# A two-layer diffusion trunk on one core: adaLN steps moved into the first norm, final states moved to w_out's transposes, other PSUM banks for the second norm, attention's first values later

## The reference

```
mod = silu(cond) @ w_ada[l] + b_ada[l]          # 6 x 1024: sh1 sc1 g1 sh2 sc2 g2
hn  = rmsnorm(x, norm_mix) * (1 + sc1) + sh1
proj = hn @ w_in[l]                             # 3840 columns, three head groups
  differential attention (8 heads) | retention (4 heads, both directions) | HGRN2 (4 heads, both)
x  += g1 * (concat of the three @ w_out[l])
hn  = rmsnorm(x, norm_ffn) * (1 + sc2) + sh2
x  += g2 * moe(hn)                              # 16 experts, top 2, gate/up/down of 1024 x 512
```

## Time and profile before

| | us |
|---|---|
| median of 3 runs | 951.66 |
| the profiled execution, whole | 953.32 |
| its span, first to last instruction | 951.5 |
| PE busy | 920.2 |
| DVE busy | 431.9 |
| ACT busy | 158.7 |
| POOL busy | 63.7 |

### The profile page before, as it was taken

One profiled execution on the slowest core, in us unless ns is written; L12 is line 12 of the kernel. 1 busy time (PEld: TensorE's weight loads), 2 busy tenths in 40 slices (PEclk: granted clock), 3 DMA queues, 4 the chain that ended last, 5 costly groups with the idle time before them and its releaser, 6 DMA issues.

```text
span 951.5 us, 13385 instructions
## 1 busy us (share of the span) xinstructions
PE 920.2 (97%) x5191; PEld 499.6 (53%) x5197; DVE 431.9 (45%) x780; ACT 158.7 (17%) x408; POOL 63.7 (7%) x96
## 2 busy tenths in 40 slices
PE   5999999999999999999999999999999999999997
PEld 2755575568553444344437556657864444443442
DVE  1385887742423122232145999876252321222223
ACT  2212024320210100010111211432021001000100
POOL 1112230020000000000000223000000000000001
PEclk9999999999999999999999999999999999999999
DMA  9996574675999999999996632601189999999993
GB/s 365 401 390 268 222 267 177 243 278 213 408 420 422 421 421 421 421 422 420 421 421 252 225 124 91 235 32 38 35 364 422 421 421 421 421 421 421 421 421 137
DMA packets 48430, 303.63 MB, mean 319 GB/s; under 512 B 7680, under 2 KB 7696, under 8 KB 14960
## 3 DMA queue, kind: packets, MB, share of 16 engines
q1 hardware_dynamic: 42368, 291.52, 75.2%
q0 software_dynamic: 2960, 8.63, 2.6%
q10 hardware_dynamic: 3040, 2.62, 0.8%
HBM read 300.10 MB, written 2.65 MB: 318 GB/s over the span
## 4 chain that ended last, share of the span: by engine, by line
PE 84%; DVE 9%; DMA 3%; ACT 2%; issue 1%; SPq 0%; DVEq 0%; ACTq 0%
PE ps L427 82%; PE ps L461 2%; DMA ring<-in_w_in 2%; ACT eP L1582 1%; DMA ring<-in_w_ada 1%; DVE fa L1263 1%; DVE rt L1057 1%; DVE eP L1361 1%; DVE stat L1057 1%; DVE xy L1257 1%; DVE eP L1359 1%; DVE hnT L1105 0%; DVE sq L1214 0%; DVE proj L1290 0%; DVE proj L1224 0%
## 5 line engine op out<-in xcount | busy, mean ns | idle before, releaser
L427 PE MATMUL ps<-ring,proj 128*64 128x512 f32 x1024 | 226.3, 595 | 1.0 <-ACT proj L1829 1.0
L427 PE MATMUL ps<-ring,hnT 128*128 128x512 f32 (+1 forms) x576 | 203.2, 505 | 2.3 <-issue 1.2
L427 PEld LDWEIGHTS ps<-ring,hnT 128*128 128x128 f32 x576 | 106.9, 191 | 75.9 <-issue 67.7
L427 PEld LDWEIGHTS ps<-ring,proj 128*64 128x64 f32 x1024 | 72.6, 137 | 132.8 <-issue 131.1
L427 PE MATMUL ps<-hnT,ring 128*64 128x128 f32 (+2 forms) x576 | 74.0, 342 | 2.9 <-DVE hnT L1105 1.6
L427 PEld LDWEIGHTS ps<-hnT,ring 128*64 128x64 f32 (+1 forms) x576 | 60.7, 160 | 13.9 <-issue 2.9
L427 PEld LDWEIGHTS ps<-proj,xs 128*128 128x128 f32 x512 | 58.4, 192 | 12.5 <-issue 11.4
L427 PE MATMUL ps<-proj 128*128 128x512 f32 x128 | 61.7, 607 | 0.0
L427 PE MATMUL ps<-proj,xs 128*128 128x128 f32 x512 | 61.4, 278 | 0.1
L1553 DVE COPY proj<-ps 128x512 f32<-128x512 f32 x16 | 11.1, 692 | 108.0 <-PE ps L427 108.0
L427 PE MATMUL ps<-ring,silT 128*32 128x512 f32 x384 | 48.8, 630 | 9.6 <-DVE silT L1073 6.9
(11 more groups left out here) (231 smaller groups left out, 920.9 us busy)
## 6 DMA issues: line engine op xcount, KB each, us to landing
ring<-in_w_gate SPq DMA_DIRECT2D x64, 1024.0 KB, 14.4
ring<-in_w_down SPq DMA_DIRECT2D x64, 1024.0 KB, 16.8
ring<-in_w_ada SPq DMA_DIRECT2D x48, 1024.0 KB, 8.6
ring<-in_w_in SPq DMA_DIRECT2D x28, 1024.0 KB, 8.5
eP<-in_w_up SPq DMA_DIRECT2D x16, 1024.0 KB, 15.8
wT<-in_w_up SPq DMA_DIRECT2D x16, 1024.0 KB, 17.9
fa<-in_w_up SPq DMA_DIRECT2D x16, 1024.0 KB, 17.7
xy<-in_w_up SPq DMA_DIRECT2D x16, 1024.0 KB, 19.1
```

What stands on the lines that cost most here:

```text
L427: ins = nc.tensor.matmul(*a, **k)
```

## The change

Six edits, in both layers unless said otherwise:

1. `AT_CHANGE` becomes (5, 1, 1): layer 1 takes five adaLN steps before the norm of g = 0 as before, one after it, and one after the norm of g = 1. The two come from behind block r, where three stood and one stays. SP loads six of them before block f of layer 1 and the seventh behind f.
2. `da_values(0, 0)` moves behind the first half of block s.
3. The final state of the retention moves, in layer 1 only, ahead of the last adaLN steps and of the first `out_of`; the final state of HGRN2 moves in both layers from the second norm to the transposes of w_out, and uses bank 1 (`b = 2 - i`).
4. The second norm's g = 1 uses banks 2 and 0, not 0 and 3.
5. ACT's copies of the states move to match, and both states are stored before the second norm.
6. One semaphore, `stored`, counts all stores.

```diff
-ADA_BEHIND = ((2, 3, 3, 3, 3, 2, 3, 2), (0, 0, 0, 0, 0, 3, 0, 0))
-AT_CHANGE = 5
+ADA_BEHIND = ((2, 3, 3, 3, 3, 2, 3, 2), (0, 0, 0, 0, 0, 1, 0, 0))
+AT_CHANGE = (5, 1, 1)
...
-                    for step in IN_CHANGE:
+                    change = iter(IN_CHANGE)
+                    for step in itertools.islice(change, sum(AT_CHANGE[0:2])):
                         load_ada(*step)
...
+                    if l and name == "f":
+                        for step in change:
+                            load_ada(*step)
...
-                    b = claim_for_norm() if h or first is None else first
+                    if banks[h] is not None:
+                        b = banks[h]
+                        pe.wait_ge(S(f"bank{b}_free"), c.claim(b))
+                    else:
+                        b = claim_for_norm() if h or first is None else first
...
-                    normalized_group("hn1", "xn1", 0, at_change)
+                    normalized_group("hn1", "xn1", 0, lambda b: at_change(0))
+                    at_change(1)
...
                         if l and g:
                             normalized_group("hn1", "xn1", 1)
+                            at_change(2)
...
-                    b = 2
+                    b = 2 - i
...
-                da_values(0, 0)
 
                 ss = open_block("s")
                 b = by_token("s", 0, 0, ss)
+                da_values(0, 0)
...
                 transposed("mix", "mixed", 0, (6, 7))
+                if l:
+                    end_state(0, "r", T_RV)
                 ada_steps(len(LATER[l]))
...
                         transposed("mix", "mixed", 1)
-                        end_state(0, "r", T_RV)
+                        if not l:
+                            end_state(0, "r", T_RV)
+                        end_state(1, "h", T_GI)
                         copied_group("mix", 1)
...
                 normalized_group("hn2", "xn2", 0)
-                end_state(1, "h", T_GI)
                 if l + 1 < L:
-                    normalized_group("hn2", "xn2", 1, lambda b: next_layers(3))
+                    normalized_group("hn2", "xn2", 1, lambda b: next_layers(3), banks=(2, 0))
                 else:
-                    normalized_group("hn2", "xn2", 1, lambda b: stream_zeros(b, 5))
+                    normalized_group("hn2", "xn2", 1, lambda b: stream_zeros(b, 5), banks=(2, 0))
...
+                if l:
+                    end_state(0, "r")
                 mixed_columns(1)
-                end_state(0, "r")
+                if not l:
+                    end_state(0, "r")
+                end_state(1, "h")
                 store_state(0, "o_ret")
+                store_state(1, "o_hg")
                 squares("xn2")
-                end_state(1, "h")
...
-                store_state(1, "o_hg", "stored_state")
```

More of the change, by code:

```diff
@@ L335, in build @@
         LATER = [[(0, "g", k) for k in range(KC)] + [(0, "y", k) for k in range(KC)] + [(1, "x", k) for k in range(KC)],
-                 [(1, "y", k) for k in range(AT_CHANGE, KC)]]
+                 [(1, "y", k) for k in range(sum(AT_CHANGE), KC)]]
         IN_ROUTER = [(1, "g", k) for k in range(KC)]
-        IN_CHANGE = [(1, "y", k) for k in range(AT_CHANGE)]
+        IN_CHANGE = [(1, "y", k) for k in range(sum(AT_CHANGE))]
         half_experts = {n: ap[n].rearrange("l e h p m -> p (l e h) m") for n in ("w_gate", "w_up", "w_down")}
@@ L482, in claim_for_norm, with normalized_group @@
                 return b
-            def normalized_group(stage, factors, g, ahead=None, first=None):
+            def normalized_group(stage, factors, g, ahead=None, first=None, banks=(None, None)):
                 xv = x[:, g].rearrange("p (k q) -> p k q", k=KC)
                 for h in range(2):
-                    b = claim_for_norm() if h or first is None else first
+                    if banks[h] is not None:
[3 more added lines that the diff above has]
+                        b = claim_for_norm() if h or first is None else first
                     if not h:
@@ L549, in next_layers, with at_change @@
                         ada_step(*step)
-                def at_change(b):
-                    for step in IN_CHANGE:
+                change = iter(IN_CHANGE)
+                def at_change(n):
+                    for step in itertools.islice(change, AT_CHANGE[n]):
                         ada_step(*step)
@@ L1619, in squares, with store @@
                         rstd(g, slice(2, 3), D, (stage + "r", g))
-                def store(dst, src, name="stored"):
-                    acte.dma_start(dst, src).then_inc(S(name), 16)
-                    led.made(name, (name,), 16)
+                def store(dst, src):
+                    acte.dma_start(dst, src).then_inc(S("stored"), 16)
+                    led.made("stored", ("stored",), 16)
                 squares("xn1")
                 acte.wait_ge(S("stored"), c.before("stored"))
-                if l:
-                    acte.wait_ge(S("stored_state"), c.before("stored_state"))
                 def modulation(l, what, norm):
@@ L1739, in end_state, with store_state @@
                     evac((name + "state",), None, name + "stateS", fn=lambda src: nc.scalar.copy(stout[:, i].rearrange("p h e -> p (h e)"), src[:, 0:256]))
-                def store_state(i, out, name="stored"):
+                def store_state(i, out):
                     for d in range(2):
-                        store(ap[out][0].rearrange("l r h d e -> r d l h e")[d, :, one(l)].rearrange("d l h e -> d (l h) e"), stout[64 * d:64 * d + 64, i], name)
+                        store(ap[out][0].rearrange("l r h d e -> r d l h e")[d, :, one(l)].rearrange("d l h e -> d (l h) e"), stout[64 * d:64 * d + 64, i])
                 def ret_columns(a, to, scale):
@@ L1841, in _ @@
             acte.wait_ge(S("stored"), c.value("stored", "end", 0) + 32)
-            acte.wait_ge(S("stored_state"), c.value("stored_state", "end", 0))
         @block.gpsimd
```

## The result

The changed kernel takes 958.49 us (median of 12 runs, 957.01 to 961.31), the kernel before, run beside it, 953.70 us (12 runs, 950.55 to 956.13). The ratio is 1.0056, interval 1.0040 to 1.0073: 5.3 us slower, between 3.8 and 7.0. The direction was as forecast and the size near it (+4.3, inside that interval); the time itself, forecast at 956.0 in a range to 957.9, was not.

What follows compares the result with a forecast made beforehand. TensorE's chain was 84%, but a saturated load stream was met first. +3.0 at f (layer 0's 0.3 included), +0.3 block s, -0.5 second norm, +1.5 clock: +4.3 on 951.66 gives 956.0, range 953.6 to 957.9.

Steps and rivals of the forecast that it cites:

- f's place in the stream: Layer 1's first norm: f's second half lands one 1 MB load, 2.5 us, later; TensorE waits 2.5 to 3.4 us.
- The stream's late start: Layer 0's second norm: HGRN2 state delays the load stream 0.93 us, o_hg stores give back 0.1; f complete at 507.1.
- The clock at f: Block f of layer 1: the wait drops TensorE's clock to 0.5, priced at 1.5 us, ends 0 and 1.9.
- Two steps less behind r: Layer 1 behind block r: 1.8 us less TensorE only lengthens the wait at v's bank to about 3.0; value 0.
- Block s: Bank turn makes modulation_by_feature wait 1.3 us in layer 1; net +0.3 us per layer, no clock drop in layer 1.
- rival B: A second clock drop, at block s of layer 1 behind the new 1.3 wait: +1.2 us more, 957.2; chance 0.12.
- The second norm: Layer 1's second norm: moved state and freed bank together give -0.5 us, ends 0 and -0.93.
- The base: Whole kernel: the +4.3 us change is added to the median of 951.66, giving 956.0; the profiled execution took 953.32.
- DMA idle: Load stream: saturated from 240 to 503 us; DMA idle anywhere between 240 and 500 would show the forecast wrong.
- 0.25 us before its use: Block f of layer 1: its second half landed at 503.5, 0.25 us before f started at 503.75.

Runs made afterwards that it cites:

- a2: The changed kernel with (4, 1, 1), so five adaLN loads before f again, and two steps behind r: 955.17 us, ratio 1.0019 to the kernel before.
- c1: The changed kernel with eleven matmuls of zeros in the wait before block f of layer 1: 957.01 us, ratio 1.0041 to the kernel before.
- a1: The kernel before with only the moved adaLN steps and their loads, (5, 1, 1) and one step behind r: 957.39 us, ratio 1.0054.
- a3: The changed kernel with da_values(0, 0) back ahead of block s: 958.25 us, ratio 1.0049 to the kernel before.
- a4: The changed kernel with layer 0's HGRN2 state and its stores back between the second norm's groups, in bank 1: 959.17 us, ratio 1.0060 to the kernel before.
- b2: The changed kernel with eight matmuls of zeros ahead of the adaLN step behind block r in layer 1: 958.15 us, ratio 1.0046 to the kernel before.
- d1: The kernel before with da_values(0, 0) behind block s's first half, plus four matmuls of zeros before modulation_by_feature, both layers: 954.58 us, ratio 1.0008.
- b6: The kernel before with only da_values(0, 0) moved behind the first half of block s: 956.38 us, ratio 1.0022.
- b3: The changed kernel with (4, 1, 1), two steps behind r, da_values(0, 0) back, layer 0's HGRN2 state back in bank 2: 953.09 us, ratio 0.9985 to the kernel before.
- b4: The kernel before with edits 3 to 6 in layer 1 alone; second norm's banks (2, 0) and layer 0's state in bank 2: 952.35 us, ratio 0.9988.

## Why the prediction was right or wrong

**f's place in the stream: right.** The wait in front of f, forecast between 2.5 and 3.4 us, was 2.57, ended by the load, and 2.30 with edit 1 alone; it went with one load less (a2). f for g = 1 came 4.30 us later against the steps ahead of it; the forecast had 3.0 - 0.3 + 1.5 = 4.2. That it fits to 0.1 is partly luck: f started 2.87 later against the steps and not 3.1, and the clock cost 0.2 more than in the sum, the norm and the second step together another 0.2. Edit 1 alone gives the ratio of the whole change within its error.

**The stream's late start: the term was mis-sized.** The release came late as forecast, but the o_hg stores gave back some 0.7 and not 0.1. So f was complete at 504.0 in an execution that stood 2.4 ahead, which is 506.4 and not 507.1 on the clock of the one before. At the 421 GB/s of the stream their 0.13 MB, in 544 packets of some 240 bytes, would take 0.3 us. The Trainium skill, "DMA: Bandwidth & Descriptors", section "Why small descriptors are slow (HBM only)", says that each packet carries a fixed overhead, which for a 256-byte descriptor is 27%. By that figure the stores would take an estimated 0.4 us. The landings show more, and no run here shows why.

**The clock at f: right.** 0.50 from 505 to 508, priced at 1.5, measured 1.67 by c1.

**Two steps less behind r: right in value, incomplete in place.** As TensorE time it is worth 0: the stretch from f to v's bank is 119.8 to 119.9 us in a1, a2, a3, a4, b2 and c1, as before, whatever TensorE does in it. But TensorE's slack did not all go to the wait at v's bank; 1.3 us of it went to a new wait for ScalarE at 609, which I had not looked for. That the clock can fall behind the longer waits (at 611 us in the changed kernel, at 634 and 636 in a1 and a3) was not in the forecast either.

**Block s: the term that was too small.** "I get +0.3", and no drop of the clock in layer 1. The wait of 1.3 us came as forecast. With the clock up the order of the banks costs 0.49 (b2, a2, d1). The profile has 1.4 + 0.45 in layer 1, with half clock, and edit 2 alone costs 2.1 us (0.6 to 3.7). That was rival B, given 0.12. In the profiled executions the clock fell at that place, between 645 and 649 us, in the changed kernel, a2, a4, b6 and c1, five of the six kernels that have edit 2 without zeros there, and in d1. But edit 2 is not the only way to it: of the seven kernels without it, b3 lost the clock there too, and a1 and a3 some 10 us earlier.

**The second norm: right**, -0.50.

**The base: the step that failed.** "I add the change to the median: 956.0." The median of 951.66 stood on three runs. The kernel before takes 950.6 to 956.1 us in the 12 runs here, and its median is 953.7. The spread goes with the clock: in the 82 runs of it beside the experiments, those with a mean granted clock of 0.989 or less took 955.1 to 957.6 us (18 runs), those with 0.994 or more 951.1 to 953.9 (9 runs). On the base of 953.7 the same sum is 958.0, 0.5 us from what was measured; so 2.0 of the 2.5 us of the miss are the base. The rest is the change, 4.8 by the medians and 5.3 by the ratio, not 4.3, and block s is the term that was short. The profiled execution, at 953.32, would have been the better base. That its 957.6 fits the 957.50 of the changed kernel's profile is luck, since that one had gained 2.4 in layer 0.

**"DMA idle" and "0.25 us before its use": read too simply.** I took one execution's margin for the kernel's. From 240 to 503 us the stream sets the earliest time at which f can start, in the kernel before too, and a part of what TensorE loses or gains in layer 0's router goes into the wait for it. That fits f's waits of 1.51 in b4 and 2.12 in d1, which have no sixth load ahead of it, and the 1.40 of b2, which was 1.40 later in the router than the changed kernel and waited 1.17 less. It has a limit: in b2 and in b6, the two with 7 us of half clock in the router, the stream itself fell to 311 and 272 GB/s from 273 to 275 us, and in b6 f did not wait for its load at all. So a stream without slack was true of the execution that I read, and need not be of the next.

## What to carry to other kernels

A step moved into a gap brings its load with it. Where the loads are one full stream, ask at which place of the stream the moved load now stands and what lands one place later; a gap of 0.7 us was filled at the price of a wait of 2.6. Take the base of a forecast from as many runs as the spread wants, and ask of every new wait whether the clock can fall behind it, since that price (1.4 to some 3 us in the profiles here) can be larger than the wait.

## What the runs showed that I had not expected

The same stretch of layer 0's router takes 11.28, 12.63 or 14.03 us in different executions, by how much of it ran at half clock. Two stores of 64 KB went with a load stream some 0.7 us longer. And the 2.6 us in front of f let the clock fall in the changed kernel, as 2.47 did in a3, 2.30 in a1 and 2.12 in d1, but 1.92 in a4 did not, nor 1.51 in b4.
